# Twelve weight sums moved from VectorE to GpSimd, and a new order in the query products and the cross attention of a streaming encoder step

## The reference

```
def cross_attention(xn, mk, mv, w_xq, xq_norm, w_xo):
    bsz, t, _ = xn.shape
    q = rmsnorm((xn @ w_xq).reshape(bsz, t, N_HEADS_X, HEAD_DIM_X), xq_norm)
    s = jnp.einsum('bqhd,bkhd->bhqk', q, mk).astype(jnp.float32) * (HEAD_DIM_X ** -0.5)
    p = jax.nn.softmax(s, axis=-1).astype(mv.dtype)
    o = jnp.einsum('bhqk,bkhd->bqhd', p, mv).reshape(bsz, t, N_HEADS_X * HEAD_DIM_X)
    return o @ w_xo
```

## Time and profile before

| what | value |
|---|---|
| median of 3 runs | 1512.80 us (1512.69 to 1513.93) |
| the profiled execution | 1512.34 us |
| its span in the profile | 1510.6 us |
| granted TensorE clock | 1.00 |
| PE busy | 1492.1 us, 99% |
| DVE, ACT, POOL busy | 1012.0, 612.3 and 244.6 us |

### The profile page before, as it was taken

How to read it: one execution, slowest core, us unless ns; L and a number is a source line. 1 busy time by engine, 2 the same in 40 slices (tenths; PEclk the granted TensorE clock), 3 DMA queues, 4 the chain that set the end, 5 groups by cost and what they waited for, 6 DMA issues and landing times.

```text
span 1510.6 us, 26930 instructions
## 1 busy us (share of the span) xinstructions
PE 1492.1 (99%) x10972; PEld 1439.9 (95%) x10972; DVE 1012.0 (67%) x1447; ACT 612.3 (41%) x1052; POOL 244.6 (16%) x322
## 2 busy tenths in 40 slices
PE   9999999999999999999999999999999999999999
PEld 8999999988779999987999999999999999999999
DVE  7646787757788449867444986666666597547653
ACT  7421032146675236445323643333334344333332
POOL 1020000002100100000000165445544210000110
PEclk9999999999999999999999999999999999999999
DMA  8434111102212531142222243443345875454663
GB/s 282 145 110 168 54 43 43 46 1 94 72 37 74 159 117 57 57 142 74 87 85 74 94 178 131 149 159 146 128 160 187 324 236 177 124 173 126 186 212 102
DMA packets 64497, 189.35 MB, mean 125 GB/s; under 512 B 7936, under 2 KB 12344, under 8 KB 64240
## 3 DMA queue, kind: packets, MB, share of 16 engines
q1 hardware_dynamic: 39824, 95.30, 19.3%
q0 software_dynamic: 24560, 92.45, 17.1%
HBM read 138.58 MB, written 54.12 MB: 128 GB/s over the span
## 4 chain that ended last, share of the span: by engine, by line
PE 91%; DVE 4%; ACT 2%; issue 1%; DMA 1%; SPq 0%; DVEq 0%; ACTq 0%
PE ps L445 32%; PE ps L3325 22%; PE ps L3301 21%; PE ps L3098 3%; PE ps L2639 2%; PE ps L2888 2%; PE ps L2939 2%; PE ps L2913 2%; PE ps L3148 1%; PE ps L3115 1%; PE ps L486 1%; DVE pt L2045 0%; DVE B_lo L2057 0%; DMA w_raw<-slabs 0%; ACT scores L1283 0%
## 5 line engine op out<-in xcount | busy, mean ns | idle before, releaser
L445 PE MATMUL ps<-A_hi,w_hi 128*128 128x364 f32 (+1 forms) x624 | 138.7, 330 | 0.3 <-DVE Y L1776 0.3
L445 PE MATMUL ps<-A_lo,w_hi 128*128 128x364 f32 (+1 forms) x624 | 137.4, 328 | 0.0
L445 PE MATMUL ps<-A_hi,w_lo 128*128 128x364 f32 (+1 forms) x624 | 136.7, 327 | 0.0
L408 ACT ACTIVATE w_hi<-w_raw 128x1024 fp32r<-128x1024 f32 x36 | 37.9, 1060 | 243.0 <-PE ps L445 140.8
L445 PEld LDWEIGHTS ps<-A_hi,w_hi 128*128 128x128 f32 x624 | 106.1, 188 | 6.1 <-issue 5.6
L445 PEld LDWEIGHTS ps<-A_lo,w_hi 128*128 128x128 f32 x624 | 107.9, 188 | 0.0
L445 PEld LDWEIGHTS ps<-A_hi,w_lo 128*128 128x128 f32 x624 | 107.7, 188 | 0.0
L3301 PE MATMUL ps<-t_hi,wq_hi 128*128 128x272 f32 x480 | 99.3, 288 | 0.2 <-issue 0.2
L3301 PE MATMUL ps<-t_lo,wq_hi 128*128 128x272 f32 x480 | 99.2, 288 | 0.0
L3301 PE MATMUL ps<-t_hi,wq_lo 128*128 128x272 f32 x480 | 99.1, 288 | 0.0
L3325 PE MATMUL ps<-r_lo_b,wq_hi 128*128 128x272 f32 x448 | 93.7, 290 | 0.0
(11 more groups left out here) (372 smaller groups left out, 3827.8 us busy)
## 6 DMA issues: line engine op xcount, KB each, us to landing
w_raw<-slabs SPq DMA_DIRECT2D x65, 512.0 KB, 3.8
quads_d<-quad_sum POOLq DMA_DIRECT2D x64, 272.0 KB, 2.9
w_raw<-wdn POOLq DMA_DIRECT2D x32, 512.0 KB, 4.0
r_raw_a<-quads_d SPq DMA_DIRECT2D x56, 272.0 KB, 2.8
r_raw_b<-quads_d SPq DMA_DIRECT2D x56, 272.0 KB, 3.3
quads_d<-hid_stage POOLq DMA_DIRECT2D x48, 272.0 KB, 2.7
Y<-xT POOLq DMA_DIRECT2D x16, 546.0 KB, 4.6
y_d<-Y POOLq DMA_DIRECT2D x16, 546.0 KB, 3.1
```

What stands on the lines that cost most here:

```text
L408: e.activation(WH[:, par], RAW[:, par], ACT.Copy).then_inc(s.w_hi, 1)
L445: ins = e.matmul(PS[:, 3 * par + c, 0:n_], wt[:, wpar, w], xt[:, col:col + n_], start=(first and n == 0 and m == 0), stop=(last and n == l ...
```

## The change

1. `q_left_sum` moves from DVE's list to POOL's. POOL runs the twelve sums one behind the other as their waits allow, in the order 1, 2, 5, 4, 8, 9, 11, 12, 15, 16, 19, 18, ahead of its loads of `y1_d`. For the second and third pair a sum waits until the low part of the one that used the same tile in the pair before is made.
2. `Q_TURN` ends 15, 14, 17, 16, 19, 18, 20. With it go waits and the places of combines, copies, scales, scores 1 and 2 and the first steps of the cross attention on all three engines; `q_add(1)` moves behind the low part of position 15, `q_squares(2)` from position 18 to 19, `q_add(2)` to 20, ahead of `xq_nrm(1, 1)`.
3. In the cross attention the dictionaries change, and in each unit the spreadings stand before the sum of squares and the values.

```
-Q_TURN = [0, 3, 1, 2, 5, 4, 7, 6] + list(range(8, 14)) + [15, 14] + list(range(16, N_QPROD))
+Q_TURN = [0, 3, 1, 2, 5, 4, 7, 6] + list(range(8, 14)) + [15, 14, 17, 16, 19, 18, 20]
...
-        X_VALUES = {1: 0, 5: 1, 7: 2, 10: 3, 14: 4, 16: 5, 18: 6}
+        X_VALUES = {1: 0, 5: 1, 8: 2, 11: 3, 13: 4, 15: 5, 18: 6}
         X_DECODE = {5: 0, 10: 1, 15: 2}
-        X_STAT, X_RECIP = 5, 6
-        X_BCAST = {3: (2, 0), 4: (2, 1), 8: (3, 0), 12: (3, 1)}
+        X_STAT, X_RECIP = 4, 6
+        X_BCAST = {2: (2, 0), 4: (2, 1), 7: (3, 0), 10: (3, 1)}
...
-        V_SPLIT = {1: 1, 4: 2, 11: 3}
+        V_SPLIT = {3: 1, 6: 2, 14: 3}
...
-            for h, n in enumerate((14, 16, 18)):
+            for h, n in enumerate((14, 17, 19)):
...
+            def q_left_sum(q):
...
+                if p and i in (1, 2, 4, 5):
+                    g.wait_ge(s.sp_lo, Q_POS[q - 7] + 1)
+                if i == 1:
+                    if p == 0:
+                        g.wait_ge(s.tile_done, S_XQ + 2)
+                    for half in range(2):
+                        g.wait_ge(w_inx[half], 16 * (p + 1))
+                    g.tensor_tensor(QSW[0][:, :], a21, a22, ALU.add).then_inc(s.sp_sum, 1)
...
             g.wait_ge(s.y1_out, 128)
+            for q in [1, 2, 5, 4, 8, 9, 11, 12, 15, 16, 19, 18]:
+                q_left_sum(q)
...
-                if n == 18:
+                if n == 19:
                     q_squares(2)
+            q_copy(16)
...
+                if u == 2:
+                    e.wait_ge(s.prod, N_QPROD)
...
-                if u == 1:
+                if u in X_DECODE:
+                    xd_hi(X_DECODE[u])
+                if u in X_VALUES:
+                    xo_hi(X_VALUES[u])
+                if u == 2:
                     q_squares(3)
                 if u == X_STAT:
                     q_root(3, bank=xt_bank(u + 1))
...
             xevac(0)
             q_left_lo(3)
             xevac(1)
-            q_left_sum(1)
-            q_left_sum(2)
             q_left_lo(1)
             q_t_lo(1)
             q_left_lo(2)
-            q_left_sum(5)
-            q_left_sum(4)
             q_left_lo(5)
             q_left_lo(4)
...
-                if n + 1 < N_QPROD:
-                    q_left_sum(Q_TURN[n + 1])
                 q_left_lo(Q_TURN[n])
+                if n == 15:
+                    q_add(1)
                 q_scale(q)
...
-                if n in (14, 19):
-                    q_add(1 if n == 14 else 2)
+                if n == 20:
+                    q_add(2)
                 if n == 18:
                     xq_nrm(1, 0, lo=0)
                 if n == 20:
                     xq_nrm(1, 1, lo=0)
...
                 if n == 18:
+                    xscores(1)
                     e.wait_ge(s.u_add, 3 * N_QPAIR - 2)
                     xq_stat(2, 0, bank=4)
                     n_rc += 1
-                    xscores(1)
                 if n == 19:
                     xtransposes(0)
-            e.wait_ge(s.u_add, 3 * N_QPAIR)
+                    e.wait_ge(s.u_add, 3 * N_QPAIR - 1)
+                    xscores(2)
             xtransposes(1)
-            xscores(2)
...
-                if u in X_VALUES:
-                    xvalues(X_VALUES[u])
+                if u in X_BCAST:
+                    e.wait_ge(s.x_olo, 2 * xvalues_before(u))
+                    pe_bcast(e, cnt, X_BCAST[u][1], rc_wait(n_rc))
                 if u == X_STAT:
...
+                if u in X_VALUES:
+                    xvalues(X_VALUES[u])
```

More of the change, by code:

```diff
@@ L1029, in _ @@
                 g.dma_start(y1_d[k], y(k)).then_inc(s.y1_out, 16)
+            def q_left_sum(q):
+                p, i = divmod(q, 7)
+                raw = q_raw(p)
+                a11, a12, a21, a22 = (raw[:, 0, 0:512], raw[:, 0, 512:1024], raw[:, 1, 0:512], raw[:, 1, 512:1024])
+                if p and i in (1, 2, 4, 5):
[6 more added lines that the diff above has]
+                    g.tensor_tensor(QSW[0][:, :], a21, a22, ALU.add).then_inc(s.sp_sum, 1)
+                elif i == 2:
+                    g.wait_ge(s.sp_sum, 4 * p + 1)
+                    g.tensor_tensor(QSW[1][:, :], QSW[0][:, :], a11, ALU.subtract).then_inc(s.sp_sum, 1)
+                elif i == 4:
+                    g.tensor_tensor(QSW[2][:, :], a11, a21, ALU.subtract).then_inc(s.sp_sum, 1)
+                elif i == 5:
+                    g.wait_ge(s.sp_sum, 4 * p + 2)
+                    g.tensor_tensor(QSW[3][:, :], a12, QSW[1][:, :], ALU.subtract).then_inc(s.sp_sum, 1)
             g.wait_ge(s.y1_out, 128)
+            for q in [1, 2, 5, 4, 8, 9, 11, 12, 15, 16, 19, 18]:
+                q_left_sum(q)
             for k in range(KT):
@@ L1435, in q_left_hi @@
                 else:
-                    e.wait_ge(s.sp_sum, 4 * p + ({1: 1, 2: 2, 5: 3, 4: 4} if p == 0 else {1: 1, 2: 2, 4: 3, 5: 4})[i])
+                    e.wait_ge(s.sp_sum, 4 * p + ({1: 1, 2: 2, 5: 3, 4: 4} if p != 1 else {1: 1, 2: 2, 4: 3, 5: 4})[i])
                 e.activation(WQ[0][:, n % 4], q_left(p, i), ACT.Copy).then_inc(s.sp_hi, 1)
@@ L1534, in xv_hi @@
                 e.wait_ge(xkv_in[h], 64)
-                e.wait_ge(s.prod, N_QPROD - 1 if h == 0 else N_QPROD)
+                e.wait_ge(s.prod, N_QPROD - 2 if h == 0 else N_QPROD)
                 e.activation(XV[0][:, h], XKV[h][:, 1], ACT.Copy).then_inc(s.x_vhi, 1)
@@ L1555, in _ @@
                     xv_hi(V_SPLIT[u])
-                if u in X_DECODE:
-                    xd_hi(X_DECODE[u])
-                if u in X_VALUES:
-                    xo_hi(X_VALUES[u])
                 if u in O_SPLIT:
@@ L2178, in q_t_lo @@
                     e.tensor_tensor(XTL[i][:, k], XTF[i][:, k], XTH[i][:, k].bitcast(F32), ALU.subtract).then_inc(s.t_lo, 1)
[L2180 to L2198, removed]
             def q_left_lo(q):
@@ L2230, in q_scale @@
                 n = QUAD[i][1]
-                e.wait_ge(s.u_add, 3 * p + i - 2)
+                e.wait_ge(s.u_add, 3 * p + (0, 1, 3, 2)[i - 2] if p == 2 else 3 * p + i - 2)
                 e.tensor_tensor(q_quad(p, i), q_quad(p, i), RSTD[:, n * HT:(n + 1) * HT], ALU.mult).then_inc(s.u_rel, 1)
@@ L2305, in _ @@
             q_combine(4)
-            q_left_sum(8)
             q_left_lo(8)
             q_combine(5)
-            q_left_sum(9)
             q_scale(3)
@@ L2313, in _ @@
             q_combine(6)
-            q_left_sum(11)
             q_left_lo(10)
@@ L2334, in _ @@
                     xq_nrm(1, 1, lo=0)
-            q_combine(17)
-            q_scale(17)
             xmin(0)
-            q_combine(18)
[L2339 to L2345, removed]
+            xnorm(0)
+            q_combine(19)
+            xmin(1)
+            q_scale(19)
+            q_mix()
+            xnorm(1)
+            q_combine(18)
             def xo_lo(q):
@@ L2370, in _ @@
             xpt_lo(0)
+            q_scale(18)
+            xmin(2)
             q_combine(20)
@@ L2373, in _ @@
             v_lo(0)
-            xmin(2)
             for u in range(N_XU):
@@ L2381, in _ @@
                     xpt_lo(u)
+                if u in X_DECODE:
+                    xd_lo(X_DECODE[u])
+                if u in X_VALUES:
+                    xo_lo(X_VALUES[u])
                 if u in V_SPLIT:
@@ L2385, in _ @@
                     q_mix()
[L2386 to L2389, removed]
                 if u in X_BCAST:
@@ L3090, in q_product @@
                 else:
-                    e.wait_ge(s.u_add, 3 * p + 2)
+                    e.wait_ge(s.u_add, 3 * p + (3 if p == 2 else 2))
                 b = bank(p, i)
@@ L3210, in _ @@
                     n_rc += 1
-                if u in X_BCAST:
-                    e.wait_ge(s.x_olo, 2 * xvalues_before(u))
-                    pe_bcast(e, cnt, X_BCAST[u][1], rc_wait(n_rc))
+                if u in X_VALUES:
+                    xvalues(X_VALUES[u])
                 if u == 17:
```

1 line of the change is left out of this document (removed).

## The result

| | before | after |
|---|---|---|
| median, us (18 executions each) | 1513.30 (1511.41 to 1514.55) | 1516.38 (1514.95 to 1522.89) |
| the profiled execution | 1512.34 | 1515.54 |

A forecast was written before the change was run, and what follows sets the result against it. PE's list was taken as the bound. Terms 2.4 - 0.15 + 0.1 = +2.4 us on the profiled 1512.34 gave 1514.8; with the median 0.46 above the profiled execution, 1515.2, range 1510.5 to 1518.5.

The forecast's parts named there:

- What bounds it: Whole kernel: PE's list bounds it, busy 1492.1 of 1510.6 us; waits from 590 to 740 us total 6.8 us.
- Part 1: Sums on POOL: turn-taking with DVE delays product 2 by 1.3 and product 6 by 1.1 us; +2.4, bounds 0 and +5.
- the sum for product 2: First pair: held DVE low parts make product 2 start at 597.2 instead of 595.88, 1.3 us lost.
- Part 2: Last pairs: two waits of 0.6 go, -0.75 each; scores 0 stall 1.6 instead of 0.25, +1.35; -0.15 in all.
- Part 3: Cross attention: old waits costing 6.4 us are relieved, new ones cost 6.5; about +0.1, bounds -4.5 and +2.
- Five stalls: Cross attention: transposes 5 wait 0.7, spreading (3, 0) 1.8, values 2 0.6, values 3 2.0, xo_part after values 5 1.4.
- my 6.4: Cross attention: cost of the old waits of 2.0, 1.6, 1.1 and 0.9, with restarts and a small one near 685.
- Covered sums: Rival at the POOL sums: no change because DVE's turns cost PE nothing, 1512.9; chance 0.18.
- The change does what it says: Rival: sums find gaps, products 2 and 6 aren't held, half of part 3's new stalls real; -3.4, 1509.4; chance 0.14.
- A hold of 1.8 for each sum: Rival, slower by more: POOL holds DVE 1.8 instead of 1.28 for each of the first eight sums; 1517.8; chance 0.18.
- Only part 1 is wrong: Rival at the POOL sums: DVE's turn costs PE nothing, 1512.9, no change; chance 0.18, as covered sums.
- The other order of POOL's sums: Rival: sum 8 falls behind low part 2, product 2 loses 0, product 6 keeps its loss; 1513.9; counted with the forecast.

The follow-up runs named there:

- first sums twice: The changed kernel with each of the first pair's four sums made twice on POOL; 1521.12 us, ratio to before 1.0053.
- second pair later: The changed kernel with POOL's sum 8 waiting until the low part of product 6 is made; 1513.48 us, ratio to before 1.0006.
- Norm first: The changed kernel with low part 20 and the norm (1,1) moved ahead of combine 17 on DVE; 1514.10 us, ratio to before 1.0008.
- sums on POOL only: The kernel before with only the twelve sums moved to POOL, old order of products and old units; 1515.62 us, ratio 1.0021.
- reordered kernel: The changed kernel with all sums on DVE, the norm (1,1) ahead of combine 17, and new cross attention units and orders; 1505.61 us, ratio to before 0.9950.
- first pair on DVE: The changed kernel with the first pair's four sums back on DVE, POOL's eight others starting behind them; 1517.10 us, ratio to before 1.0031.
- the first experiments: Not listed as such; apparently those measured beside 1512.79 us of the kernel before: sums on POOL only, orders only, cross units only, first pair on DVE.
- cross units only: The kernel before with only the cross attention's new units for spreadings, values and value splits; 1513.76 us, ratio 1.0005.
- orders only: The changed kernel with all twelve sums back on DVE, so only the new product order and cross attention units; 1513.20 us, ratio to before 1.0001.

## Why the prediction held, step by step

- **What bounds it.** As forecast. PE's work is unchanged to 0.2 us, and the differences in the stretches are its waits and the slower start behind each.
- **Part 1, +2.4, measured +2.74.** The mechanism is shown: POOL's and DVE's operations take turns where DVE reads two SBUF tiles, the loss follows the number of sums in the stretch (first sums twice) and goes when they move out of it (second pair later). The low parts of 1.2 to 1.8 us, the wait before product 2 and the wait of product 6 for combine 4 are the signs that the forecast named. The terms: product 2 starts 10.46 us behind product 0, before 9.05, so 1.41 for 1.3. But it isn't one loss: 0.49 of it comes at product 3, which the forecast didn't name. Product 3 waits for the read of the second plain tile, which stands behind low part 3 with its 1.23 for 0.69. Before, that read ended at 588.34 + 1.29 = 589.63, 0.2 us ahead of product 3:

```profile
586.83 0.41 PE L3098 MATMUL ps<-A_hi,wq_hi 128*128 128x272 f32 x2
...
589.85 0.41 PE L3098 MATMUL ps<-A_hi,wq_hi 128*128 128x272 f32 x2
```

  These are the starts of products 0 and 3 before, 3.02 apart; after it is 590.83 - 587.32 = 3.51. I had laid this read to its end at 590.1 and not asked who waits for it; that the sum for product 2 came out at 1.3 all the same is in part luck, since at product 2 itself only 0.9 were lost. Product 6: (611.11 - 597.78) - (607.94 - 595.88) = 1.27 for 1.1, restart with it. Combine 4 started 22.97 behind product 0 where 22.8 was laid out, so the holds together were right to 0.2, far from the bound of 1.8 for each.
- The Trainium skill (GPSIMD Engine Reference, 8. Key points) names DVE instructions with two SBUF inputs, and all that was held here is of that kind; an operation that reads PSUM was not held (589.40). On POOL's side a copy with one input holds DVE too, as measured above.
- **Part 2, -0.15, measured -0.26.** Both waits of 0.6 went and scores 0 wait 1.41 where 1.6 was laid out (the terms given there, 4.5 less 3.0, make 1.5). Norm first shows that combine 17 and what follows it ahead of the norm are the cause: with them moved, the stall is gone and B shorter by 1.57.
- **Part 3, +0.1, measured +0.32 in C.** Five stalls were forecast as 0.7, 1.8, 0.6, 2.0 and 1.4; measured are 0.21, 1.74, 0.57, 2.08 and 1.20, at the places named. Mis-sized is the first, the wait for the root of head 3, by 0.5. The sum of 5.8 is less than 6.5 and C is longer all the same, because the old stalls were over-sized by more: the four waits are 2.00 + 1.57 + 1.08 + 0.85 = 5.5 in PE's timeline before, and my 6.4 took in their restarts, which I left out of the new sum, and one near 685 that no row of the waits has. In the waits alone it is 5.5 before and 5.8 after, +0.3, about the +0.32 of C. What the restarts add on either side wasn't separated.
- **The sum.** +2.4 forecast; +2.8 in the stretches, +3.2 in the profiled execution, +3.1 in the medians. What stands above the forecast in the profiled execution is 0.3 of part 1, 0.2 of part 3, less 0.1 of part 2, and 0.5 by which the stretch began later (587.32 for 586.83), where the change touches nothing; less 0.1 elsewhere. The median of 1516.38 is 1.2 above the expected 1515.2: 0.5 of it because the kernel before itself came out at 1513.30 here and not at 1512.80, 0.7 because the change cost 3.1 and not 2.4. The clock, which the forecast doesn't speak of, has a part in these medians (last section).
- **The chances.** The likeliest outcome by the forecast was "same" (0.48), with 0.38 for slower. Its bound for slower, 1515.8, lay 0.6 above the expected time, and the median fell 0.6 beyond the bound, at 1.0023 against 1.002, with an interval that reaches to either side. So the mechanism and the place of the loss came as forecast, but the side of the 0.2% on which the time fell had the smaller chance.
- **The rivals.** Covered sums (no held DVE operation) fell to the 5.93 of the first pair. "The change does what it says": its 6.8 us were there, as the reordered kernel shows with 7.0 in B and C, but part 3 exchanged stalls for stalls and part 1 added its own. A hold of 1.8 for each sum would make a DVE operation take 2.2 us a turn; the turn was 1.75 at most. "Only part 1 is wrong" falls with the sums on POOL only, which lost as much. The other order of POOL's sums didn't occur: sum 8 started at 594.13, before low part 2.
- **In an experiment** the same slip as at product 3 came once more, larger: for the first pair on DVE I priced each wait by itself, and didn't see that product 6 waits for the end of one list, whatever lies ahead in it.

## What to carry to other kernels

Moving work from an engine that isn't the bound to an idle one gains nothing by itself, and on this pair of engines it can cost: for every operation moved to POOL ask which of DVE's operations on SBUF run at that time and who waits for them; put it where DVE has slack (here one wait on DVE's progress gave back 2.2 of 2.7 us). Price a run of stalls on one list at the last event that waits for that list's end, not one by one. And when an order is changed to remove a stall, lay out the next late event behind each: here six stalls went and nine came, and only the versions in which each was followed to its end were faster.

## What the runs showed of the hardware

**Turns.** Whole instructions alternate where DVE's has two inputs in SBUF: beside POOL's sums of 1.6 to 1.8 us a DVE subtraction of 544 columns takes up to 1.75 us a turn instead of 0.64, and POOL's own operation goes from 1.30 to 1.79. A one-input copy of POOL (0.62) does the same on a smaller scale. A DVE operation that reads PSUM took its usual 1.28 beside a sum.

**The clock behind a wait.** Some executions show a stretch at PE's lower level of 1.2 GHz shortly behind an idle moment, in a kernel that is 99% busy. Busy time by stretch (after the window: length, PE, PEld, DVE, ACT, POOL with instructions, the granted clock, DMA) around values 3, which wait 2.1 us in both kernels; first after, then the cross units only, and of that the middle of the slow stretch by itself:

```profile
700.00:710.00 10.00, 7.92 (x45) 6.71 (x44) 6.95 (x15) 5.10 (x13) 1.06 (x2) 1.00 0.37 112
```

```profile
700.00:710.00 10.00, 8.46 (x34) 7.04 (x35) 6.22 (x13) 4.21 (x11) 0.53 (x1) 0.83 0.36 112
703.00:706.00 3.00, 3.00 (x9) 2.32 (x8) 0.07 (x1) 0.00 (x0) 0.53 (x1) 0.50 0.34 71
```

A clock of 0.50 is the lower level. Of the second row, a third of the time stands at the lower level: fewer matmuls (34 for 45) in more busy time. It costs 1.5 us: C is 71.39 there, 71.44 in the orders only, and 69.89 in after, with the same waits. The sums on POOL only has such a stretch too, behind the wait of 2.0 for `xq_nrm(2, 0)` (granted clock 0.56 from 680 to 683 us), and it costs only 0.56: C is 70.13 for 69.57 before. There the wait of 0.9 for xpt_hi, which followed in before, is not among its waits: PE, slower, came to values 1 later. The first pair on DVE shows it behind the wait of 2.12 before product 6, and first sums twice behind that of 4.08:

```profile
611.00:620.00 9.00, 9.00 (x64) 8.41 (x62) 5.41 (x9) 1.45 (x3) 3.02 (x2) 0.81 0.15 60
```

```profile
600.00:610.00 10.00, 9.60 (x57) 9.61 (x58) 10.00 (x10) 5.22 (x8) 6.47 (x4) 0.70 0.01 2
```

The Trainium skill (TensorE: Matmul & The Clock Gate, What's actually happening) has these two levels too and ties them to how busy PE has just been; the rows agree in that the clock fell only behind such waits, or, before the 4.08 ended, within it.

In this stretch of the profiled executions of before and of after there is none, and whether one comes behind a given wait of 2 us differs between executions. The mean granted clock of every execution is on record, and it goes with the time. Of the 18 of after, the nine with a clock of 1.000 took 1514.95 to 1516.46 us (median 1515.54), the nine with 0.996 to 0.999 took 1516.31 to 1522.89 (median 1517.35). Of 28 of the kernel before, taken with the first experiments, 16 had 1.000 (median 1512.58) and 12 less (median 1513.12). So such stretches go with about 0.8 us of after's median and 0.2 of before's, and among the executions at 1.000 after is still 3.0 us slower. In which place of the other executions the clock fell isn't on record. The kernels with almost no waits scatter least (reordered 1505.10 to 1506.22, clock 1.000 in all five), which fits, with few executions. A stall of 2 us that such a stretch follows has a price of up to 3.5 us, and that isn't in a sum of waits.
